# Setting the small products of a block scan between the large ones on TensorE

## What is computed

```python
u_a, z_a, b_c, c_c, h_c, z_c, g_a, g_c = split(x @ w_in)
# state space, per group: h[t] = lam * h[t-1] + bb @ u[t];  y[t] = Re(C h[t]) + D u[t]
y = gelu(y); y = y * sigmoid(y @ w_glu)
y_a = (y * silu(z_a)) @ w_out_a
y_c = (b_c * conv3(c_c * h_c) * silu(z_c)) @ w_out_c
out = (sigmoid(g_a) * y_a + sigmoid(g_c) * y_c) @ w_o
x = layernorm(alpha * x + out)
```

## Time and profile before

| | us |
|---|---|
| median of three runs | 1627.57 |
| lowest, highest | 1622.84, 1632.72 |
| the profiled execution | 1623.52 |
| its span in the trace | 1621.7 |
| mean granted TensorE clock, share of full speed | 0.976 |
| PE busy | 1570.0 (97%) |
| DVE busy | 769.2 (47%) |
| ACT busy | 402.2 (25%) |

### The profile page before, as it was taken

One profiled execution on the slowest core, in us unless ns is written; L12 is line 12 of the kernel. 1 busy time (PEld: TensorE's weight loads), 2 busy tenths in 40 slices (PEclk: granted clock), 3 DMA queues, 4 the chain that ended last, 5 costly groups with the idle time before them and its releaser, 6 DMA issues.

```text
span 1621.7 us, 26870 instructions
## 1 busy us (share of the span) xinstructions
PE 1570.0 (97%) x11852; PEld 1565.4 (97%) x11852; DVE 769.2 (47%) x1014; ACT 402.2 (25%) x498; POOL 188.4 (12%) x348
## 2 busy tenths in 40 slices
PE   8999999999999999999999999999999999999990
PEld 8999999999999999999999999999999999999990
DVE  5976373464463552632523533223733455343438
ACT  4222222222122222222222122223421222221214
POOL 0110031121211211311213112010000000000000
PEclk9999999999999999999999999999999999999995
DMA  8352262452443534634625434254544343232312
GB/s 304 108 154 91 89 170 73 115 144 88 125 119 95 154 98 122 171 109 124 165 75 164 123 115 140 88 157 140 174 156 134 126 139 115 93 110 91 125 46 116
DMA packets 78084, 204.42 MB, mean 126 GB/s; under 512 B 18704, under 2 KB 19216, under 8 KB 77968
## 3 DMA queue, kind: packets, MB, share of 16 engines
q1 hardware_dynamic: 62096, 172.00, 33.2%
q0 software_dynamic: 15872, 30.70, 8.0%
HBM read 169.77 MB, written 28.16 MB: 122 GB/s over the span
## 4 chain that ended last, share of the span: by engine, by line
PE 92%; DVE 5%; SPq 1%; issue 0%; DMA 0%; ACT 0%; DVEq 0%
PE acc L582 87%; DVE r_all L1369 1%; DVE w_lo L881 1%; DVE r_all L1368 1%; SPq L385 1%; PE y_ps L626 0%; PE y_ps L627 0%; PE y_ps L625 0%; PE y_ps L624 0%; DMA w_raw<-in_w 0%; PE y_ps L623 0%; PE v_ps L603 0%; PE v_ps L602 0%; PE y_ps L622 0%; PE v_ps L601 0%
## 5 line engine op out<-in xcount | busy, mean ns | idle before, releaser
L582 PE MATMUL acc<-xh,w_hi 128*128 128x288 f32 x2560 | 557.0, 299 | 11.1 <-DVE w_lo L881 11.1
L582 PE MATMUL acc<-xl,w_hi 128*128 128x288 f32 x2560 | 554.9, 298 | 0.0
L582 PE MATMUL acc<-xh,w_lo 128*128 128x288 f32 x2560 | 554.8, 298 | 0.0
L881 DVE TENSOR_TENSOR w_lo<-w_raw,w_hi 128x1024 fp32r<-128x1024 f32 x232 | 283.8, 1224 | 441.8 <-ACT w_hi L692 440.4
L582 PEld LDWEIGHTS acc<-xh,w_hi 128*128 128x128 f32 x2560 | 416.6, 191 | 13.1 <-DVE w_lo L881 7.4
L582 PEld LDWEIGHTS acc<-xh,w_lo 128*128 128x128 f32 x2560 | 416.9, 191 | 0.0
L582 PEld LDWEIGHTS acc<-xl,w_hi 128*128 128x128 f32 x2560 | 416.4, 191 | 0.0
L692 ACT ACTIVATE w_hi<-w_raw 128x1024 fp32r<-128x1024 f32 x232 | 245.3, 1057 | 645.0 <-PE acc L582 629.4
L582 PE MATMUL acc<-mh,w_hi 128*128 128x288 f32 x512 | 110.1, 296 | 0.0
L582 PE MATMUL acc<-mh,w_lo 128*128 128x288 f32 x512 | 109.9, 295 | 0.0
L582 PE MATMUL acc<-ml,w_hi 128*128 128x288 f32 x512 | 109.9, 295 | 0.0
(11 more groups left out here) (266 smaller groups left out, 1501.0 us busy)
## 6 DMA issues: line engine op xcount, KB each, us to landing
w_raw<-in_w SPq DMA_DIRECT2D x232, 512.0 KB, 3.7
sg_dram<-out_st SPq DMA_DIRECT2D x32, 288.0 KB, 4.5
v_sw<-v_st POOLq DMA_DIRECT2D x32, 144.0 KB, 4.9
gc_in<-sg_dram SPq DMA_DIRECT2D x16, 288.0 KB, 2.8
sz_in<-sg_dram SPq DMA_DIRECT2D x16, 288.0 KB, 2.8
x_in<-in_xT SPq DMA_DIRECT2D x16, 288.0 KB, 2.8
outT<-o_st SPq DMA_DIRECT2D x16, 288.0 KB, 2.1
mb<-mq_dram POOLq DMA_DIRECT2D x8, 512.0 KB, 6.6
```

The source lines that it names most:

```text
L582: ins = pe.matmul(acc[:, par, t, 0:TH], w, m[:, k0 + k, t * TH:(t + 1) * TH], start=first and k == 0 and n == 0, stop=last and k == KH - 1 ...
L881: dve.tensor_tensor(w_lo[h % NW][:, :], w_raw[:, h % NW, :], w_hi[h % NW][:, :].bitcast(F32), ALU.subtract).then_inc(lo_ready, 1)
```

## The change

PE no longer does the small products as pieces of their own. `half` takes a list `beside`, and after each of its 24 pairs it emits at most one small product and at most one tap:

- `states_in`: after every second pair of the halves at offsets 9 and 10, 12 in each.
- `taps`, now a function of its own: after every third pair of the half at offset 10. At four of these eight places a product of `states_in` goes ahead of the tap.
- `outputs`: after two of every three pairs of the halves at offsets 19, 20 and 21, 16 in each.

The other engines' steps move: ACT's `lch`, `lbh` and `uh` go to offset 7 (from 3 and 4), DVE's `lbl` and `ul` to 8 (from 5), `lcl` to 9 (from 4), the evacuation of `v_ps` to 11 (from 7), `chunk_sums` to 12 (8), the first exchange to 12 (9), `scan` to 13 (11), the second exchange to 13 (12), `k_hi` to 13 (9), `k_lo` to 14 (10), `store_k` to 14 (11), `load_lt` to 15 (13), `turn_back` to 15 (14), `hh` to 16 (15), the evacuation of `y_ps` to 22 (19) and the steps behind it by three. `Y_LOAD` is 152; from then on two pieces of `y` are loaded, and from h = 154 to 157 split, in each half. `turn_table` gets a wait that its place in the order fulfils.

```diff
-Y_LOAD = SSM0 + SSM_PER * (BLK - 1) + 23
+Y_LOAD = SSM0 + SSM_PER * (BLK - 1) + 24
...
+            if h == Y_LOAD:
+                sp.wait_ge(y_made, BLK)
+                sp.wait_ge(y_stored, U_LOAD * (BLK - 1))
+                load_y(0)
+                load_y(1)
+            if Y_LOAD + 2 <= h < Y_LOAD + 5:
+                load_y(2 * (h - Y_LOAD) - 2)
+                load_y(2 * (h - Y_LOAD) - 1)
...
-            if (b := ssm_step(h, 11)) is not None:
+            if (b := ssm_step(h, 14)) is not None:
                 store_k(b)
-            if (b := ssm_step(h, 13)) is not None:
+            if (b := ssm_step(h, 15)) is not None:
                 load_lt(b)
...
+                    for emit, b, part in beside:
+                        emit(b, part, 3 * k + n)
...
+        def states_in(b, part, at):
+
+            if part == 0 and at == 0:
+                pe.wait_ge(lbl_ready, b + 1)
+                pe.wait_ge(ul_ready, b + 1)
+                if b:
+                    pe.wait_ge(v_evac, b)
+            if at % 2:
+                return
+            g, m = divmod(12 * part + at // 2, 3)
+            w, u = ((lbh, uh), (lbh, ul), (lbl, uh))[m]
+            ins = pe.matmul(out_of(v_ps, g), w[:, g, :], u[:, g, :], start=m == 0, stop=m == 2)
...
+        def taps(b, part, at):
+
+            if at == 0:
+                pe.wait_ge(lc_ready, b + 1)
+                if b:
+                    pe.wait_ge(y_evac, b)
+            if at % 3:
+                return
+            g = at // 3
...
+        def outputs(b, part, at):
...
+            if at % 3 == 2:
+                return
+            g, m = divmod(16 * part + at // 3 * 2 + at % 3, 6)
...
-            if (b := ssm_step(h, 7)) is not None:
-                states_in(b)
-            if (b := ssm_step(h, 19)) is not None:
-                outputs(b)
+            beside = [(emit, b, part) for emit, off, part in ((states_in, 9, 0), (states_in, 10, 1), (taps, 10, 0),
+                                                              (outputs, 19, 0), (outputs, 20, 1), (outputs, 21, 2))
+                      if (b := ssm_step(h, off)) is not None]
...
-            half(h, par, xh, xl, h % 2 * KH, h % 2 == 0, h % 2 == 1)
+            half(h, par, xh, xl, h % 2 * KH, h % 2 == 0, h % 2 == 1, beside=beside)
```

More of the change, by code:

```diff
@@ L570, in fresh, with half @@
             used[par] += 1
-        def half(h, par, mh_, ml_, k0, first, last, per_block=None):
+        def half(h, par, mh_, ml_, k0, first, last, per_block=None, beside=()):
             pe.wait_ge(lo_ready, h + 1)
@@ L592, in out_of @@
             return ps[:, t, at:at + CH]
[L594 to L603, removed]
-            ins.then_inc(v_done, 1)
-            pe.wait_ge(lc_ready, b + 1)
-            if b:
-                pe.wait_ge(y_evac, b)
-            for g in range(NG):
-                x, q = divmod(g, 4)
-                ins = pe.matmul(y_ps[32 * q:32 * q + 32, 0, x * P:(x + 1) * P], bbar[:, g, :],
-                                lc[:, g, 0:T, :].rearrange("p t c -> p (t c)"), start=True, stop=True)
-            ins.then_inc(k_done, 1)
@@ L614, in outputs @@
[L614 to L628 removed]
+        def states_in(b, part, at):
[9 more added lines that the diff above has]
+            ins = pe.matmul(out_of(v_ps, g), w[:, g, :], u[:, g, :], start=m == 0, stop=m == 2)
+            if (g, m) == (NG - 1, 2):
+                ins.then_inc(v_done, 1)
@@ new lines, in taps @@
+        def taps(b, part, at):
[6 more added lines that the diff above has]
+            g = at // 3
+            x, q = divmod(g, 4)
+            ins = pe.matmul(y_ps[32 * q:32 * q + 32, 0, x * P:(x + 1) * P], bbar[:, g, :],
+                            lc[:, g, 0:T, :].rearrange("p t c -> p (t c)"), start=True, stop=True)
+            if g == NG - 1:
+                ins.then_inc(k_done, 1)
@@ new lines, in outputs @@
+        def outputs(b, part, at):
+            if part == 0 and at == 0:
+                pe.wait_ge(hl_ready, b + 1)
+                pe.wait_ge(lcl_ready, b + 1)
+                pe.wait_ge(lt_loaded, LT_LOAD * (b + 1))
+                pe.wait_ge(k_evac, b + 1)
+            if at % 3 == 2:
+                return
+            g, m = divmod(16 * part + at // 3 * 2 + at % 3, 6)
+            ch, cl = (t[:, g, :, :].rearrange("p t c -> p (t c)") for t in (lch, lcl))
+            w, v = ((lth[:, g, :], uh), (lth[:, g, :], ul), (ltl[:, g, :], uh), (ch, hh), (ch, hl), (cl, hh))[m]
+            ins = pe.matmul(out_of(y_ps, g), w, v[:, g, :], start=m == 0, stop=m == 5)
+            if (g, m) == (NG - 1, 5):
+                ins.then_inc(y_done, 1)
@@ L1049, in turn_table @@
         def turn_table(b):
+            if b:
+                dve.wait_ge(st_ready, b)
             gs = slice(b * NG, (b + 1) * NG)
@@ L1129, in scan_steps @@
                 output_matrix(b)
-            if (b := ssm_step(h, 4)) is not None:
+            if (b := ssm_step(h, 8)) is not None:
+                dve.wait_ge(lbh_ready, b + 1)
+                dve.tensor_tensor(lbl[:, :, :], mb[:, :, :, :].rearrange("p g c s -> p g (c s)"),
+                                  lbh[:, :, :].bitcast(F32), ALU.subtract).then_inc(lbl_ready, 1)
+                dve.wait_ge(uh_ready, b + 1)
+                dve.tensor_tensor(flat(ul), flat(u_raw), flat(uh).bitcast(F32), ALU.subtract).then_inc(ul_ready, 1)
+            if (b := ssm_step(h, 9)) is not None:
                 dve.wait_ge(lch_ready, b + 1)
```

89 lines of the change are left out of this document (32 added, 57 removed).

## The result

| us | before | changed |
|---|---|---|
| median | 1628.52 (4 runs) | 1702.28 (4 runs) |
| lowest, highest | 1622.84, 1632.72 | 1696.48, 1708.54 |
| profiled execution, its span | 1623.52, 1621.7 | 1708.54, 1706.7 |

The changed kernel is slower: the ratio is 1.0456, with a 95% interval from 1.0407 to 1.0505. The direction is that of the forecast (1647), the size is not; 1702 lies outside the range of 1622 to 1665.

The account below looks back on a forecast made before the run. The prediction took PE, 97% busy, to bound the kernel. From the profiled execution, 1623.5 - 15 - 1 + 25 + 6 + 5 - 4 + 7 = 1646.5, forecast as 1647 us, range 1622 to 1665.

Parts of the forecast that it names:

- Part 5: At `outputs`: PE waits 0 to 4 us for late reads, taken as 1 in each of five blocks, +5 us.
- Part 1: At `outputs` and the half behind: spreading small products ends the loss to the low clock, -15 us.
- third rival: At `outputs`: reads land 3 to 4 us late and the clock falls again, +18, so 1665 us; chance 0.12.
- Part 2: Small products between large ones: weight load only moves to the other side, cost nearly unchanged, -1 us.
- second rival: Small products: weights loaded further ahead under the previous large matmul, -30, so 1617 us; chance 0.08.
- Part 3: Half at offset 10: each lone tap's change of tile width drains the array, 3.1 a block, +25 us.
- first rival: Taps do not drain the array one by one: +8 in place of +25, so 1630 us; chance 0.15.
- Part 4: At `states_in`: PE waits 0.75 us in each block for ACT's and DVE's later roundings, +6 us.
- the prediction's own sign of being wrong: Wrong if the half at offset 10 takes under 10 us, or waits in `outputs` are over 3 us.
- Part 6: At `H_GLU`: earlier pieces of `y` remove PE's 2.4 us stop and some 1.6 of low clock, -4 us.
- Part 7: Large halves: 46 that took 6.24 us after clock falls go to 6.40, +7 us.
- fourth rival: The pace turns fast, all halves at 6.24 us including 95 slow ones left: 1624 us, the same; chance 0.12.

Follow-up runs that it names:

- the kernel with three repairs: Changed kernel with the next block's matrices issued at offset 12, the taps in one place, and the roundings for `states_in` one half earlier: 1616.69 us, ratio 0.992.
- the kernel with the store ahead: The kernel with three repairs, plus `k_hi` at offset 12, `k_lo` at 13 and `store_k` ahead of the second exchange: 1612.36 us, ratio 0.9885.

## Why the prediction was right in direction and wrong in size

The direction was right for the reason given: without the 64 us of Part 5 the kernel would still be 1% slower, by the taps.

**Part 1, the clock (-15).** Right where PE doesn't wait. Block 7 of the changed kernel has 1.00, and so have all eight in the kernel with three repairs. Against the kernel before that is 15.2. One reading was wrong: in blocks 0 and 6 the clock fell while the piece was still running, 4.0 and 3.0 us after its start, and not behind all 5.3 of it. In the changed kernel itself none of it was to be had in blocks 0 to 6, because each wait in `outputs` brought a fall of its own, 17 us in all. My third rival said just this ("longer waits and the clock falls again"), but priced it at 18 us.

**Part 2, the small products (-1).** Right. Three halves with 48 small ones take 24.41 in block 7. ACT's starts in that block:

```profile
1116.01 1.06 ACT L708 ACTIVATE w_hi<-w_raw 128x1024 fp32r<-128x1024 f32 x1 [4.57 <-PE acc L587]
1124.08 0.65 ACT L821 ACTIVATE out_st<-acc 128x576 f32<-128x576 f32 x1 [7.01 <-PE acc L587]
1132.29 1.06 ACT L708 ACTIVATE w_hi<-w_raw 128x1024 fp32r<-128x1024 f32 x1 [6.32 <-PE acc L587]
```

That leaves 24.41 - 3 x 6.40 = 5.21 for the 48, and the piece took 5.36 (48 x 0.111, and 0.03): -0.14 a block. The second rival, loads pulled further ahead, is ruled out: at 0.06 less for each of 16 it wanted these halves at some 7.1.

**Part 3, the taps (+25).** Right, and for the reason given: 11.62 in the half at offset 10 (11.6 forecast). Without their wait, the halves that hold `states_in` and the taps are 25.1 us longer over the program than in the kernel before, and 26.1 longer than in the run that puts the taps together. The first rival, taps that don't drain the array, falls with it; the wide ones show the drain is the change of width.

**Part 4, the wait at `states_in` (+6).** Right: eight waits, 7.4 us by the table, 7.6 by the halves at offset 9 once the roundings come earlier.

**Part 5, the waits at `outputs` (+5). This is the step that failed.** It cost 64, of them 47 in waits and 17 at the low clock, and the prediction's own sign of being wrong, waits of over 3 us in `outputs`, is there in all seven. The term's place, its engine and its instruction were right, the size was wrong by a factor of 13, from three steps of its working:

- "with 1.3 MB of matrices ahead of them in the queue I add 2 to 3": they add some 14 us to the reads in the kernel before. The sum had let the issues of the matrices disappear under `k_lo`'s 4.6, and had taken the 15.3 us of issues from the earlier trace rows, where no matrices stood ahead. In fact POOL's own issues stop until earlier DMAs have landed: 4.26 at the second matrix, then 5.91, 3.28 and 4.78 in the reads. In block 4 the reads begin 9.1 us after the exchange and not 6.7, and their issues take 22.4 and not 15.3. From the exchange to the last read I had 27; it took 34.3. The row that could have told me stands in the earlier trace rows itself, a stop of 2.44 "issue" at the end of 16 reads: the 15.3 already held 6.9 us of such stops, so DMAs set ahead of the reads could not be free.
- "I take 1 in each of the five blocks": the price was only the wait. Each of the seven waits (3.7 to 9.5 us) came with a fall of the clock, as Part 6 had worked out for another place with 1.6 us; it is 17/7 = 2.4 here. Waits of 2.1 to 2.4 us had one in the run with the matrices early, and none in the run with three repairs and in the last one.
- "In `H_G` ... there is no wait": blocks 5 and 6 waited 8.2 and 7.7.

The own range I gave Part 5 (0 to 20) reached not a third of the way. The bound had to come from the place where nothing hides it: all the matrices' issues, and all the time in which they move, ahead of the reads.

**Part 6, the end of `y` (-4).** Right: half 160 follows half 159 by 6.40 with no gap, where before it took 10.44. The run that puts the last piece back shows the 2.4 of the stop; the fall of the clock behind it did not come in that run.

**Part 7, the pace (+7).** In the changed kernel no half takes 6.24; those without small products or waits take 6.40, as forecast. Why is not shown, and the reason that I gave, that the clock would not fall, did not hold: it fell seven times and the pace stayed at 6.40 all the same. That the term came out is luck. It is 9.7 us by the traces and not 7: the kernel before has some 60 halves at 6.24, 15 of them near its start, which the term left out. The fourth rival's 95 slow halves are wrong too; the kernel before has 150 at 6.40, which would have put that rival at 1616 and not at 1624.

With each term as the two traces have it, the sum is 1623.5 - 15.2 - 1.2 + 25.1 + 7.6 + 64.2 - 4.0 + 9.7 = 1709.7, beside the profiled execution's 1708.5; the rest lies at the program's start and end. In the kernel with the store ahead Parts 3, 4 and 5 are gone, and 1623.5 - 15.2 - 1.2 - 4.0 + 9.7 = 1612.8 is left, beside its 1612.4. What the change could give, about 1%, it gave once the steps around it stood in another order.

## What to carry to other kernels

When a step is moved behind others in a DMA queue that already stops between issues (rows with "issue" in brackets, each ending at the landing of an earlier DMA), its delay can be most of the time in which the queue works off what is ahead; bound the term by that, and add what a stop of PE does to the clock. Look also at how much earlier the step is now asked for. Small products with another tile width than their neighbours belong together in one place, since each lone tap here cost 0.27 us more than one of the same width as its neighbours, while the products of the same width cost the same wherever they stood. To keep the clock up it was enough here to break the long run of small products into three pieces, which leaves the order of the other engines nearly as it was.

## What the runs showed of the hardware that I had not expected

- **POOL's issues stop until earlier DMAs have landed.** Issues follow each other by 0.53 us, and then one comes late, by up to 9.1 us; all 95 such stops of over 0.25 us up to 1110 us, in the traces of the kernel before and the changed one, end within 0.4 us behind a landing. The same 16 reads take 15.3 us to issue with only the exchange ahead, and 24.2 in the run of the kernel before with four matrices ahead as well (1.25 MB by the page's sizes; 548.80 to 572.98). Whether bytes, the number of DMAs or something else sets how much can be on its way is not shown.
- **One piece in eight leaves the clock alone.** In the run with one piece, the same 48 small products at the same place in the block took the clock down in seven blocks and not in the eighth; three pieces of 16 never did.
- **Two paces.** Large products run at 6.40 us a half for hundreds of us, or at 6.24, both at a granted clock of 1.00. In these runs a long stretch of 6.24 (over 40 halves) came only in the kernel before and the one with its matrices moved, behind the stop at `H_GLU` and its fall of the clock; most falls were followed by 6.40. Five halves of 6.24 stand near the start in five traces, those two among them; there the kernel before goes on at 6.24 up to its first `states_in`. What chooses the pace is open.
